# One-hot products of the experts' weights in fp32r with high and low shares side by side, low parts of 80 weight tiles on GpSimd, and a new spread of the first table's products

## The reference, cut to what matters

```python
def one_block(hb):
    q = (hb @ w_q).reshape(PEER_BLOCK, PEER_HEADS, 2, PEER_HALF)
    sc = jnp.einsum('thcd,hcnd->thcn', q, sub_keys).astype(jnp.float32)
    s1, i1 = lax.top_k(sc[:, :, 0], PEER_TOPK)
    s2, i2 = lax.top_k(sc[:, :, 1], PEER_TOPK)
    ...
    top_s, pos = lax.top_k(cand_s, PEER_TOPK)
    idx = jnp.take_along_axis(cand_i, pos, axis=-1)
    g = jax.nn.softmax(top_s, axis=-1)
    u = u_tab[idx]
    act = jax.nn.gelu(jnp.einsum('thkd,td->thk', u, hb))
    wts = (g * act.astype(jnp.float32)).astype(hb.dtype)
    v = v_tab[idx]
    return jnp.einsum('thk,thkd->td', wts, v)
```

## Time and profile before

| | before |
|---|---|
| median of 3 runs | 3441.31 us (3436.02 to 3441.43) |
| profiled execution | 3439.4 us, span 3437.6 us |
| mean granted TensorE clock | 0.964 |
| TensorE busy | 3283.5 us, 96% of the span |
| VectorE busy | 1851.7 us, 54% |
| ScalarE busy | 1245.4 us, 36% |
| GpSimd busy | 330.9 us, 10% |

### The profile page before, as it was taken

The page is one execution under the profiler, slowest core; times in us unless marked ns, Lnnn a source line. Parts: engine busy times, 40 slices in busy tenths (PEclk is TensorE's granted clock), DMA queues, the critical chain, the costliest instruction groups (busy, mean ns, idle before and its releaser), DMA issues.

```text
span 3437.6 us, 37735 instructions
## 1 busy us (share of the span) xinstructions
PE 3283.5 (96%) x14948; PEld 2679.9 (78%) x14948; DVE 1851.7 (54%) x3358; ACT 1245.4 (36%) x1802; POOL 330.9 (10%) x449
## 2 busy tenths in 40 slices
PE   8989999999999999999999999999999977899999
PEld 6767776778888878888788888887888855678887
DVE  5653544447777776664555555553333477433332
ACT  4653454332222235565322222223222333532221
POOL 0000000000000008885000000000000043000000
PEclk9999999999999999999999999999999986699999
DMA  4222111323443345777855555542222310022221
GB/s 140 91 94 88 56 56 65 117 90 127 145 136 125 124 148 147 196 200 201 302 193 192 193 191 192 190 149 74 98 98 94 112 56 13 13 74 98 98 93 67
DMA packets 271199, 424.22 MB, mean 123 GB/s; under 512 B 144816, under 2 KB 148400, under 8 KB 271024
## 3 DMA queue, kind: packets, MB, share of 16 engines
q1 hardware_dynamic: 271024, 421.80, 37.6%
HBM read 348.87 MB, written 72.88 MB: 123 GB/s over the span
## 4 chain that ended last, share of the span: by engine, by line
PE 87%; DVE 6%; ACT 5%; issue 1%; DMA 1%; SPq 0%; ACTq 0%
PE pb L534 27%; PE pb L536 27%; PE pb L535 27%; PE pb L809 3%; ACT scr L1037 2%; PE pb L561 1%; DVE S L1456 1%; DVE ST L1464 1%; ACT S L1040 1%; DVE ST L1456 1%; ACT L1037 1%; DVE whl L1456 1%; ACT whl L1040 0%; DVE ST L1540 0%; DVE scr L1460 0%
## 5 line engine op out<-in xcount | busy, mean ns | idle before, releaser
L534 PE MATMUL pb<-H,whl 128*128 128x512 f32 x2432 | 1000.1, 411 | 35.3 <-DVE H L1456 18.4
L1456 DVE TENSOR_TENSOR whl<-raw,whl 128x1024 fp32r<-128x1024 f32 (+4 forms) x550 | 637.2, 1166 | 603.1 <-ACT whl L1040 601.0
L535 PE MATMUL pb<-H,whl 128*128 128x512 f32 x2432 | 961.2, 395 | 0.0
L536 PE MATMUL pb<-H,whl 128*128 128x512 f32 x2432 | 960.9, 395 | 0.0
L1040 ACT ACTIVATE whl<-raw 128x1024 fp32r<-128x1024 f32 (+4 forms) x550 | 547.7, 1004 | 471.5 <-PE pb L536 471.3
L534 PE MATMUL pb<-S,whl 128*128 128x512 f32 (+1 forms) x1700 | 662.9, 390 | 18.6 <-DVE whl L1456 11.6
L535 PE MATMUL pb<-S,whl 128*128 128x512 f32 (+1 forms) x1700 | 660.9, 389 | 0.0
L536 PE MATMUL pb<-S,whl 128*128 128x512 f32 (+1 forms) x1700 | 660.4, 388 | 0.0
L534 PEld LDWEIGHTS pb<-H,whl 128*128 128x128 f32 x2432 | 467.0, 192 | 128.0 <-DVE H L1456 21.6
L536 PEld LDWEIGHTS pb<-H,whl 128*128 128x128 f32 x2432 | 465.0, 191 | 100.3
L535 PEld LDWEIGHTS pb<-H,whl 128*128 128x128 f32 x2432 | 467.5, 192 | 85.9 <-issue 2.7
(11 more groups left out here) (173 smaller groups left out, 2589.6 us busy)
## 6 DMA issues: line engine op xcount, KB each, us to landing
raw<-in_pu SPq DMA_DIRECT2D x128, 512.0 KB, 4.0
raw<-in_pv SPq DMA_DIRECT2D x128, 512.0 KB, 4.5
raw<-in_w_in SPq DMA_DIRECT2D x72, 512.0 KB, 3.6
ad<-scr SPq DMA_DIRECT2D x128, 256.0 KB, 4.2
gd<-ST SPq DMA_DIRECT2D x8, 4096.0 KB, 21.2
GA<-gd SPq DMA_DIRECT2D x60, 512.0 KB, 4.6
GA<-ad SPq DMA_DIRECT2D x60, 512.0 KB, 6.2
raw<-in_wg SPq DMA_DIRECT2D x44, 512.0 KB, 3.4
```

The source lines that it names most:

```text
L534: e.matmul(o, lh, h, start=start, stop=False, skip_group_check=True)
L535: e.matmul(o, lh, l, start=False, stop=False, skip_group_check=True)
L536: return e.matmul(o, ll, h, start=False, stop=stop, skip_group_check=True)
L1456: return e.tensor_tensor(o, x, y, op)
```

## The change

1. **One-hot products.** The share moves from the second row to the first and is split in a high part (`high_t`, a ScalarE copy to fp32r) and a low part (`lows`, VectorE). For each token there is one fp32r matmul of 256 columns: the second index's row of ones as weights, and as moving operand the first index's row times the high share beside the same row times the low share. The two halves of the result are added on the way out of PSUM by a VectorE reduction (line 1794), which takes the place of ScalarE's copy. For three tokens of a group GpSimd makes the first index's row of ones (line 2018) and ScalarE multiplies it by the high and by the low share (line 1299, six instructions); for the fourth VectorE makes both products (line 1491), and one instruction for the four rows of the second index (line 1486). Rows and shares have two buffers, PSUM pairs three. There is one `g` step for a group of four.
2. **Low parts on GpSimd** (line 2003): all 16 units `w_pq`, the units `pu` 0 to 47, and every fourth from 48 to 116.
3. **The spread of the u steps:** 384 while the choice runs (48 for each head instead of 80), 38 as before, 536 through the one-hot products, 66 behind them. `unit_order` takes the order of the units from this list.

```diff
+def pool_makes_low(unit):
+    name, i, _ = unit
+    return name == "w_pq" or name == "pu" and (i < 48 or i < 120 and i % 4 == 0)
...
             out.append(("pq", h, c))
-            u(16)
+            u(7 if c else 9)
             out.append(("sk", h, c))
-            u(8)
+            u(5 if c else 3)
         for step in (("cand", h), ("best", h), ("pick", h, 0), ("pick", h, 1)):
             out.append(step)
-            u(8)
+            u(6)
...
-    for q in range(3):
+    for q in range(2):
         out.append(("rows", q))
     for q in range(128):
-        if q + 3 < 128:
-            out.append(("rows", q + 3))
-        for k in range(4 * q, 4 * q + 4):
-            out.append(("g", k))
-            if k % 4 == 3 and q:
-                out.append(("put", q - 1))
-            u((k + 1) * left // 512 - k * left // 512)
+        if 0 < q < 127:
+            out.append(("rows", q + 1))
+        out.append(("g", q))
+        if q:
+            out.append(("put", q - 1))
+        u((q + 1) * left // 128 - q * left // 128)
...
# TensorE
-                        last = e.matmul(b[:, c], hot2[n % 4][:, c], hot1[n % 4][:, c], start=True, stop=True, skip_group_check=True)
+                        n = step[1]
+                        b = gbank[n % 3]
+                        q.wait_ge(dve, ("put", n - 3) if n > 2 else ("top", 15))
+                        q.wait_ge(dve, ("hot2", n))
+                        q.wait_ge(act, ("share", n))
+                        for u in range(4):
+                            last = e.matmul(bank[b + u // 2][:, 256 * (u % 2):256 * (u % 2) + 256],
+                                            hot2[n % 2][:, 128 * u:128 * u + 128], share[n % 2][:, 256 * u:256 * u + 256],
+                                            start=True, stop=True, skip_group_check=True)
...
# ScalarE
-                    elif what == "put":
...
-                        copy(stage[n // 16 % 2][:, :, 4 * g:4 * g + 4].rearrange("p i u -> p u i"),
-                             bank[gbank[n % 4]].rearrange("p (u i) -> p u i", u=4)).then_inc(act.up(("put", n)), 1)
+                    elif what == "rows":
+                        n = step[1]
+                        if n > 1:
+                            q.wait_ge(prod, ("g", n - 2))
+                        else:
+                            q.wait_ge(dve, ("over", 2))
+                        q.wait_ge(pool, ("hot1", n))
+                        q.wait_ge(act, "share_hi")
+                        for u in range(3):
+                            for part in range(2):
+                                s = (high_share, low_share)[part](4 * n + u)
+                                last = e.activation(hot_share(n, u, part), hot1[n % 2][:, 128 * u:128 * u + 128], ACT.Copy, scale=s)
+                        last.then_inc(act.up(("share", n)), 1)
...
# VectorE
+                        if n > 1:
+                            q.wait_ge(prod, ("g", n - 2))
+                        tt(hot2[n % 2].rearrange("p (u i) -> p u i", u=4), iota.unsqueeze(1).to_broadcast([128, 4, 128]),
+                           I2[:, 4 * n:4 * n + 4].unsqueeze(2).to_broadcast([128, 4, 128]), ALU.is_equal)
+                        k = 4 * n + 3
+                        ts(hot_share(n, 3, 0), iota, I1[:, k:k + 1], ALU.is_equal, high_share(k), ALU.mult)
+                        ts(hot_share(n, 3, 1), iota, I1[:, k:k + 1], ALU.is_equal, low_share(k), ALU.mult).then_inc(
+                            dve.up(("hot2", n)), 1)
+                    elif what == "put":
...
+                        e.tensor_reduce(stage[n // 16 % 2][:, :, 4 * g:4 * g + 4].rearrange("p i u -> p u i"),
+                                        pb_t[:, b:b + 1024].rearrange("p (u e i) -> p u i e", u=4, e=2), AX_X, ALU.add
+                                        ).then_inc(dve.up(("put", n)), 1)
...
# GpSimd
+            def split(upto):
+                while lo_done[0] < min(upto, len(units)):
+                    j = lo_done[0]
+                    lo_done[0] += 1
+                    if pool_makes_low(units[j]):
+                        q.wait_ge(w_hi, j + 1)
+                        e.tensor_tensor(wlo(j), raw(j), f(whi(j)), ALU.subtract).then_inc(pool_lo.up(("low", j)), 1)
+            def experts():
+                for step in choice:
+                    what = step[0]
+                    if what == "pq":
+                        split(unit_at["w_pq", 2 * step[1] + step[2]] + NW - 1)
+                    elif what == "u" and step[1] % 8 == 0 and step[1]:
+                        split(unit_at["pu", step[1] // 8] + NW - 1)
+                    elif what == "rows":
+                        n = step[1]
+                        q.wait_ge(dve, ("over", 1))
+                        if n > 1:
+                            q.wait_ge(act, ("share", n - 2))
+                        for u in range(3):
+                            last = e.tensor_scalar(hot1[n % 2][:, 128 * u:128 * u + 128], iota,
+                                                   I1[:, 4 * n + u:4 * n + u + 1], None, ALU.is_equal)
+                        last.then_inc(pool.up(("hot1", n)), 1)
```

More of the change, by code:

```diff
@@ L69, in unit_order @@
     u += [("w_out", m, 1024) for m in range(8)]
-    U = [("pu", i, 1024) for i in range(128)]
-    for j in range(16):
-        u += [("w_pq", j, 1024), U.pop(0), U.pop(0), ("sk", j, 128), U.pop(0)]
-        if j % 2:
-            u += [U.pop(0) for _ in range(4)]
-    u += U
+    for step in peer_order():
+        if step[0] == "pq":
+            u += [("w_pq", 2 * step[1] + step[2], 1024)] + [("pu", 0, 1024)] * (step[1:] == (0, 0))
+        elif step[0] == "sk":
+            u += [("sk", 2 * step[1] + step[2], 128)]
+        elif step[0] == "u" and step[1] % 8 == 0 and step[1]:
+            u += [("pu", step[1] // 8, 1024)]
     for g in range(16):
@@ L381, in build @@
         ST_t, _ = at("ST", 16384, F32, offset=s_off)
-        scr_t, _ = at("scr", 10 * 512, F32)
-        pad_t, _ = at("pad", 2 * 544, F32)
+        scr_t, scr_off = at("scr", 10 * 512, F32)
+        share_t, _ = at("share", 2048, F32R, offset=scr_off + 4 * 1536)
+        high_t, _ = at("high", 512, F32R, offset=scr_off + 4 * 1024)
+        pad_t, pad_off = at("pad", 2 * 544, F32)
+        hot_t, _ = at("hot", 2 * 544, F32R, offset=pad_off)
         cst_t, _ = at("cst", NC_, F32)
@@ L416, in build @@
         units = unit_order()
+        unit_at = {u[:2]: j for j, u in enumerate(units)}
         def region(o, n):
@@ L431, in wlo, with low @@
             return whi(j, 1024 + o, n or units[j][2])
+        def low(j):
+            return pool_lo if pool_makes_low(units[j]) else w_lo, ("low", j)
         prod, act, dve, pool = signal("pe_products"), signal("act_results"), signal("dve_results"), signal("pool_results")
         w_hi, w_lo = signal("weight_high_parts"), signal("weight_low_parts")
+        pool_lo = signal("weight_low_parts_of_pool")
         w_in = [signal(f"weights_landed{i}", 16) for i in range(NRAW)]
@@ L470, in build, with hot_share, high_share, low_share @@
         I1v, I2v, TSv = (z.rearrange("p (b h k) -> p b h k", b=4, h=8) for z in (I1, I2, TS))
-        hot1 = scr[3:7]
-        hot2 = [pad[0][:, 0:512], pad[1][:, 0:512], cos_t[:, 0:512], cos_t[:, 512:1024]]
+        hot1 = [cos_t[:, 384 * i:384 * i + 384] for i in range(2)]
+        hot2 = [hot_t[:, 544 * i:544 * i + 512] for i in range(2)]
+        share = cut(share_t, 2, 1024)
+        lows = [cos_t[:, 768:1024], sm_t[:, 0:256]]
         stage = [ST[:, 8192 * i:8192 * i + 8192].rearrange("p (i t) -> p i t", i=128) for i in range(2)]
-        gbank = [4, 5, 2, 3]
+        gbank = [4, 6, 2]
+        def hot_share(n, u, part):
+            return share[n % 2][:, 256 * u + 128 * part:256 * u + 128 * part + 128]
+        def high_share(k):
+            return f(high_t[:, k:k + 1])
+        def low_share(k):
+            return lows[k // 256][:, k % 256:k % 256 + 1]
         def ga(p):
@@ L1737, in experts @@
                         q.wait_ge(prod, ("over", z))
-                        then(e.tensor_copy((I1, I2, TS)[z], bank[6]), ("over", z))
+                        if z < 2:
+                            then(e.tensor_copy((I1, I2)[z], bank[6]), ("over", z))
+                        else:
+                            q.wait_ge(act, "share_hi")
+                            for i in range(2):
+                                last = tt(lows[i], bank[6][:, 256 * i:256 * i + 256], f(high_t[:, 256 * i:256 * i + 256]), ALU.subtract)
+                            then(last, ("over", 2))
```

74 lines of the change are left out of this document (25 added, 49 removed).

## The result

The changed kernel takes 3499.23 us (median of 4 runs, 3497.46 to 3500.67) against 3439.04 for the kernel before beside it: a ratio of 1.0175, 95% interval 1.0158 to 1.0193. So it is slower, as forecast, but by 60 us and not by 24, and 4 us outside the range.

A forecast was written before the change was run, and what follows sets the result against it. TensorE's program, plus waits a change opens, was taken as the bound. Terms -55.5 + 53 + 19 + 4 + 3 = +23.5 us on 3439.4 gave 3463, so a median of 3465 us; 8-in-10 range 3425 to 3495.

The forecast's parts named there:

- products: One-hot products: 512 single fp32r matmuls at 0.120 us replace products of 0.228 us; -55.5 us.
- waits in the one-hot stretch: TensorE waits at 16 places because GpSimd's low part stands ahead of the rows ScalarE needs; +53 us, 3.3 each.
- clock behind them: One-hot stretch: the clock falls to about half speed behind 12 of 16 waits, 1.6 us each; +19 us, bounds 0 and 40.
- softmax: TensorE's wait at the softmax grows, with fewer steps to cover VectorE's chain; +3 us.
- The 4 us for VectorE's rows: One-hot stretch: at 10 places where VectorE makes the low part, its rows are done at 4.3, needed at 3.9; +4 us.
- a cheap queue: Rival: GpSimd's low part, rows and ScalarE's products at their lower bounds, waits of 34 us; 3433 us, faster; chance 0.17.
- no waits: Rival: ScalarE finds the rows ready because GpSimd runs ahead of the boundary; 3393 us; chance 0.06.
- VectorE as the bound of this stretch: Rival: the strided reduction makes VectorE need 3.5 us a one-hot group against 3.33; 3477 us; chance 0.06.
- The choice otherwise. 0: The choice: VectorE's chain of about 29 us fits TensorE's 31.3 us per head; 0 us, bounds 0 and 40.
- the two signs of being wrong: Line 831's waits summing to under 30 us, or idle TensorE at each head of the choice.
- the third rival: In the choice, GpSimd's low parts and VectorE's two-SBUF-input operations stand in each other's way; 3495 us; chance 0.11.

The follow-up runs named there:

- experiment 9: Changed kernel with the edits of experiment 6, plus each 4 MB store of the one-hot result sent as four pieces, four products apart: 3394.7 us, ratio 0.9874.
- experiment 4: Changed kernel's new spread and GpSimd low parts, but with the one-hot products, rows and copies of the kernel before: 3459.8 us, ratio 1.0065.
- experiment 1: Changed kernel with the one-hot stretch's 16 low parts one place later in GpSimd's queue, behind the next group of rows: 3429.3 us, ratio 0.9972.
- 2: Changed kernel with the 16 low parts of the one-hot stretch made by VectorE again, those of the choice still on GpSimd: 3419.8 us, ratio 0.9948.
- experiment 7: Changed kernel with GpSimd making each of the one-hot stretch's 16 low parts twice, one behind the other: 3537.2 us, ratio 1.0287.
- experiment 10: Changed kernel's new products alone: spread of the kernel before, all low parts on VectorE: 3471.3 us, ratio 1.0097.
- Experiment 3: Changed kernel with the low parts of the choice's eight odd query units back on VectorE: 3487.45 us.
- experiment 5: Changed kernel with ScalarE copying each head's odd query before it makes the next unit's high part: 3491.4 us.
- experiment 6: Changed kernel with low parts of the one-hot stretch and odd query units on VectorE, and odd query copied before the next high part: 3403.8 us, ratio 0.9901.
- 8: Changed kernel's new products and GpSimd low parts, with the spread of steps of the kernel before: 3512.0 us, ratio 1.0215.

## Why the forecast went as it did

Here is the sum again, beside what the traces give. The measured column is made of idle and busy time: experiment 9 has TensorE busy 428.3 us for the same steps and products.

| term | forecast | measured | from |
|---|---|---|---|
| products | -55.5 | -53.1 | 428.3 us against the 481.4 worked out for before |
| waits in the one-hot stretch | +53 and +4 | +57.6 | 520.3 less 462.7 us busy; 55.9 for ScalarE, 1.6 for VectorE |
| clock behind them | +19 | +34.4 | 462.7 against 428.3 us busy |
| softmax | +3 | +2.7 | 7.06 against 4.41 us |
| the choice | 0 | +14.6 | 7 x (1.00 + 0.22) + 8 x (0.54 + 0.22) |
| the rest | 0 | +1.9 | what is left to the spans, 58.1 us |

The 481.4 us were never run in one kernel: they take 0.68 us for each step that moved. Against experiment 4, which has the old products at the same spread (484.9 us), the new ones give 56.6.

**Right, in place and size:** the products at 0.12 us; the wait that GpSimd's queue opens, its 16 places (2.45 to 4.37 us each, 55.9 us in all by the timeline's rows) and its cause. Experiments 1 and 2 take the cause away in two ways, and 7 doubles it. The 4 us for VectorE's rows came to 1.6. The durations behind it were worked out from other shapes, and came within 0.05 us for the low part, and nearer for the rows, ScalarE's products and the reduction. The rivals of a cheap queue and of no waits are out; VectorE as the bound of this stretch is out too, and would have been right only with the old spread (experiment 10).

**The step that failed is "The choice otherwise. 0".** It measured 14.6 us, and idle TensorE at each head is one of the two signs of being wrong that the prediction had named. It had two faults. It held VectorE's chain to fit by about 2 us and put the picks' two-input operations clear of GpSimd's low parts, by a count of steps; in the trace the low part of the odd query unit begins at 777.02, 0.8 us after four of them, and holds them for 2.1 us. That made TensorE 1.22 us late, so some 0.9 us were in hand and not 2. This is the third rival, which had 0.11: right in the mechanism, priced at 4.7 us less 2 in hand and a fall of the clock for each head, where it costs 1.22 us and no clock. The second fault was in no case at all. I followed what the new spread does to VectorE's chain, but not what it does to ScalarE's order, where the high part of a unit waits for a buffer that a cut unit gives up later. Experiment 3 removes the one, 5 the other, and 6 both.

**The clock term was mis-sized.** The mechanism was right (half speed behind a wait), the size was not: the earlier trace rows gave 1.6 us a fall, at 12 places, 19 us, and the busy time holds 34.4. The clock fell at 15 of the 16 places; after the wait of 2.53 us at 1568.16 it stayed at 1.00. At half speed the matmuls of 512 columns start 0.43 us apart instead of 0.23. At seven of the 15 places half speed is over in under four microseconds, as behind 1187.77, and costs the 1.6 us of the forecast. At the other eight TensorE works at half speed for 4.6 to 6.2 us, as behind 1155.18, and loses 2.2 to 2.9. That is some 32 us, and 16 times the 0.22 us of experiment 5 are 3.5 more. The earlier trace rows had the price right for their waits of 2.6 us: the window behind the first of them is at full speed again.

```profile
110.00:114.00 4.00, 4.00 (x19) 3.26 (x19) 2.37 (x3) 3.12 (x4) 0.00 (x0) 0.99 0.43 127
```

What the rows before did not show is the longer fall. The length of the wait does not tell which it will be: one of 3.09 us that ended at 1441.78 gave the long one, one of 3.09 us that ended at 1628.52 the short one.

Together these two, 14.6 and 15.4 us, are 30 of the 35 us that the sum was short. The result lies only 4 us outside the range because the range was wide; the sum left one term out and had another at little over half of its size.

**The parts of the change, one by one.** Products alone +33 us (experiment 10); low parts on GpSimd and the new spread without the products +22 (4); products and GpSimd without the spread +74 (8); all three +61; all three without GpSimd's low parts in the one-hot stretch -18 (2). In these runs the products' 55 us came only with the spread that gives VectorE more TensorE time per product, and the low parts in GpSimd's queue are what turned that gain into a loss.

What stays open: the 1.9 us of the rest, of which 1.7 lie behind the last one-hot product; the 1.7 and 3.3 us by which experiments 5 and 3 gave more than their waits; and what decides whether the clock falls behind a wait, and for how long. The wait of 7 us at the softmax is in every version with the new spread, and no experiment was made on it.

## What to carry to other kernels

Before a piece of work moves to an engine with time to spare, look at what stands behind it in that engine's queue: on an engine with nearly half its time free, a second piece of 2.4 us cost TensorE 2.3 us more at each of 16 places, and moving the piece one place back in the same queue gave 70 us. A new order has to be followed on every engine that keeps one, ScalarE and SyncE too; here the first held a copy of 0.6 us and the second a store of 256 KB behind one of 4 MB. And where a bound has next to no slack by a count of steps, that is a term, not a zero.

## What the runs showed of the hardware

- While GpSimd subtracts two SBUF tiles of 128x1024 (2.39 us), VectorE's tensor_tensor and tensor_scalar with SBUF inputs do not slow down in proportion: one that starts in that time ends only after GpSimd's has ended. A tensor_tensor of 128x128 took 2.37 us instead of 0.29 and one of 128x512 2.72 instead of 0.69, both begun in GpSimd's first 0.3 us. Two tensor inputs are not needed for it: a tensor_scalar of 128x128 took 2.48 us instead of 0.34 (at all of its ten meetings in the one-hot stretch), and ended 0.08 us behind GpSimd. Beside a pair of such subtractions (795.52 to 800.27) a tensor_tensor with one PSUM input kept its 0.69 us and MAX8 and FIND_INDEX8 their 0.29. The Trainium skill (GPSIMD Engine Reference, Specifications) has the SBUF interfaces as shared between the two, with contention where VectorE reads two SBUF inputs or works in a 2-port mode. The tensor_tensor rows agree; no run here shows which mode the tensor_scalar was in. That the hold lasts for GpSimd's whole instruction is from these rows.
- An idle gap of TensorE costs 0.22 us more than its shown length, in three pairs of kernels (0.54 us cost 0.76, 1.00 cost 1.22). Most of that is in how a gap is counted, from the end of the last record: in a full stream of 512 columns the next matmul starts 0.16 us before that end (0.39 and 0.23).
- The loss of clock hardly grows with the wait: 34.4 us for 57.6 us of idle time at 16 places, 35.4 for 94.5 (experiment 7). Nor is the wait's length all that decides. In the changed kernel one of 2.45 us (1283.66) brought the clock to 0.50 and one of 2.53 us (1568.16) left it at 1.00; in experiment 1 one of 2.54 us (1286.64) left it at 1.00, one of 2.00 us (1573.91) brought it to 0.50; in experiment 6 one of 2.22 us left it at 1.00 and one of 3.47 brought it to 0.50. Waits of 1.55 us and less (experiment 10) never did. What else decides stays open.
- A store of 4 MB in pieces of 256 bytes takes 21.4 us to land by the page, and held the issue of the next transfer on SyncE's queue for 15.9 to 18.8 us behind each of seven such stores (experiment 6). In four pieces, four products apart, the longest hold of a store of the activations beside the one-hot products was 4.4 us (experiment 9).
